# Moving half of an input projection's weight loads out of the key/value stage

## The reference, cut to what matters

```python
h = rms_norm(x, g_in)
proj = h @ w_in                      # w_in: 1024 x 3008, the weights that this change moves
c_q, c_kv, k_pe, z_a, cb, cc, cx, z_c = split(proj, [256, 128, 64, 512, 512, 512, 512, 512])
q  = rms_norm(rms_norm(c_q, g_cq) @ w_uq, g_q)         # 4 heads of 128 + 64 (rotary)
kv = rms_norm(c_kv, g_ckv) @ w_ukv                     # keys and values, 8192 rows
o_attn = causal_block_attention(q, k, v)
y_attn = rms_norm(o_attn * silu(z_a), g_oa)
u = causal_depthwise_conv(cc * cx, conv_w)             # three taps
y_conv = rms_norm(cb * u * silu(z_c), g_oc)
x = x + concatenate([y_attn, y_conv]) @ w_o
return x + sigmoid(rms_norm(x, g_pl) @ w_plg) * (p_i @ w_pl)
```

## Time and profile before

| | |
|---|---|
| time, median of 2 runs | 1702.0 us (1700.94 to 1703.05) |
| profiled execution: its time | 1699.79 us |
| profiled execution: span of the slowest core (core 4) | 1698.3 us |
| spans of the 8 cores | 1692.3 to 1698.3 us |
| mean granted TensorE clock of the cores | 0.814 to 0.822 of full speed |
| key/value stage on core 4 | about 60 to 338 us |
| iteration m = 0, from its first load to the start of attention | about 338 to 454 us |

### The profile page before, as it was taken

One profiled execution on the slowest core, in us unless ns is written; L12 is line 12 of the kernel. 1 busy time (PEld: TensorE's weight loads), 2 busy tenths in 40 slices (PEclk: granted clock), 3 DMA queues, 4 the chain that ended last, 5 costly groups with the idle time before them and its releaser, 6 DMA issues.

```text
span 1698.3 us, 22578 instructions; the slowest of 8 cores (1692.3 to 1698.3 us)
## 1 busy us (share of the span) xinstructions
PE 1101.1 (65%) x5973; PEld 572.1 (34%) x6060; DVE 952.5 (56%) x1560; ACT 964.3 (57%) x1668; POOL 89.8 (5%) x144
## 2 busy tenths in 40 slices
PE   0254556454786743898674478887764488988775
PEld 0243445322443321444332242333332243333332
DVE  5476777546662326477332557777223657777632
ACT  0465577542583434388444437887444258988644
POOL 1023233300000000000000000000000000000000
PEclk9967677665887866899796789998886589999888
DMA  2556554010241110000012000000111000000011
GB/s 68 159 188 222 185 180 141 17 48 0 77 147 57 43 62 1 1 1 1 32 57 74 1 1 1 1 1 25 35 41 62 1 1 1 1 1 1 32 41 40
DMA packets 27148, 87.05 MB, mean 51 GB/s; under 512 B 4464, under 2 KB 7792, under 8 KB 27024
## 3 DMA queue, kind: packets, MB, share of 16 engines
q1 hardware_dynamic: 27024, 85.61, 15.1%
HBM read 77.21 MB, written 8.39 MB: 50 GB/s over the span
## 4 chain that ended last, share of the span: by engine, by line
DVE 31%; PE 27%; ACT 19%; issue 14%; DMA 6%; DVEq 1%; ACTq 1%; SPq 1%; POOL 0%; POOLq 0%
PE bk L382 24%; DVE racc L352 15%; ACT pt L349 5%; DMA xt<-x_kv 3%; PE bk L389 3%; ACT gt L349 2%; DMA xo<-x_own 2%; ACT e L349 2%; DVEq L157 1%; DVE ssqkn L379 1%; ACT sjk L349 1%; ACT x1b L349 1%; DVE sq L352 1%; ACT sj L349 1%; ACT sqj L349 1%
## 5 line engine op out<-in xcount | busy, mean ns | idle before, releaser
L349 ACT ACTIVATE pt<-bk,zerob,rstdk 128x512 bf16<-128x512 f32 (+3 forms) x640 | 432.5, 716 | 67.5 <-PE bk L382 22.9
L352 DVE TENSOR_TENSOR racc<-racc,pt 128x512 f32<-128x512 f32 (+3 forms) x624 | 380.6, 610 | 114.2 <-DVE racc L352 59.0
L382 PE MATMUL bk<-pt,Vp 128*128 128x512 bf16 (+3 forms) x629 | 221.5, 352 | 56.6 <-ACT pt L349 46.3
L382 PE MATMUL bk<-QrT,KrT 128*128 128x512 bf16 (+3 forms) x634 | 230.4, 363 | 1.7 <-issue 0.8
L382 PE MATMUL bk<-QpT,KcT 128*128 128x512 bf16 (+3 forms) x621 | 224.5, 362 | 4.9 <-ACT rbc L349 3.7
L382 PEld LDWEIGHTS bk<-pt,Vp 128*128 128x128 bf16 x640 | 62.4, 97 | 232.4 <-issue 224.6
L382 PE MATMUL bk<-xTh,w_own 128*128 128x260 bf16 (+1 forms) x768 | 122.1, 324 | 5.8 <-ACT ccs L367 4.2
L382 PEld LDWEIGHTS bk<-xTh,w_own 128*128 128x128 bf16 x768 | 78.6, 103 | 48.9 <-issue 9.0
L382 PE MATMUL bk<-w_o,idb 128*128 128x512 bf16 x244 | 87.7, 519 | 2.0 <-issue 1.8
L349 ACT ACTIVATE sqj<-xt 128x1024 bf16<-128x1024 f32 x64 | 67.3, 1052 | 34.4 <-DMA xt<-x_kv 30.9
L382 PEld LDWEIGHTS bk<-QrT,KrT 128*128 128x128 bf16 x640 | 63.7, 100 | 65.6 <-issue 9.8
(11 more groups left out here) (189 smaller groups left out, 1662.5 us busy)
## 6 DMA issues: line engine op xcount, KB each, us to landing
xt<-x_kv SPq DMA_DIRECT2D x64, 512.0 KB, 4.8
xo<-x_own SPq DMA_DIRECT2D x16, 512.0 KB, 4.3
xr<-x_own SPq DMA_DIRECT2D x16, 512.0 KB, 4.2
out_own<-outst SPq DMA_DIRECT2D x16, 512.0 KB, 3.0
wst<-w_in SPq DMA_DIRECT2D x8, 752.0 KB, 6.3
wst_b<-w_in SPq DMA_DIRECT2D x8, 752.0 KB, 5.4
wst<-w_o SPq DMA_DIRECT2D x8, 512.0 KB, 4.1
wst<-w_plg SPq DMA_DIRECT2D x8, 512.0 KB, 4.0
```

The lines of the kernel that those rows point to most:

```text
L349: return S.op("act", lambda e: e.activation(**kw), reads, writes, sig)
L352: return S.op(eng, lambda e: e.tensor_tensor(out=out_, in0=in0, in1=in1, op=op), reads, writes)
L382: return S.op("pe", lambda e: e.matmul(out_, lhsT=lhsT, rhs=rhs, start=start, stop=stop), reads, writes, sig)
```

## The change

The second-half job of each of the 8 chunks leaves `job_list` for a list `late_jobs`. `job_list` keeps 10 jobs. In iteration m = 0 one staging buffer `wl` (128 x 1504, f32) is allocated ahead of the x buffers. The first late load is issued before the x loads of that iteration. After that each `late_consume` scales one job into `w_own` on DVE and issues the next load into the same `wl`. Two are consumed before `rope_tables`, three after A1b, and three after A1.

```diff
+    late_jobs = []
...
-        job_list.append((rows[:, 1504:3008], 1504, [(w_own[:, c, 1312:2816], 0, 1504)], g_in_pp[:, c:c + 1]))
+        late_jobs.append((rows[:, 1504:3008], 1504, [(w_own[:, c, 1312:2816], 0, 1504)], g_in_pp[:, c:c + 1]))
...
+        if m == 0:
+            wl = A("wl", [128, 1504], F32)
+            sl_wl = S.slot("wl")
+            late_state = dict(k=0)
+            def late_issue():
+                k = late_state["k"]
+                if k < len(late_jobs):
+                    src_ap, ncols, pieces, gain_ap = late_jobs[k]
+                    S.dma(lambda e: e.dma_start(out=wl[:, 0:ncols], in_=src_ap), sl_wl, (), [wl])
+            def late_consume():
+                k = late_state["k"]
+                if k >= len(late_jobs):
+                    return
+                src_ap, ncols, pieces, gain_ap = late_jobs[k]
+                for dst, lo, hi in pieces:
+                    ts("dve", dst, wl[:, lo:hi], gain_ap, None, ALU.mult, None, [wl, gain_src], [wdst_buf])
+                late_state["k"] = k + 1
+                late_issue()
+            late_issue()
...
         if m == 0:
+            late_consume()
+            late_consume()
             rope_tables(poso_i, 16, cosQ, sinQ)
...
         run_pipelined([cq_chain()] + [za_tile(s) for s in range(4)], skew=2, maxlive=3)
         AR.release(mQ1)
+        if m == 0:
+            for _ in range(3):
+                late_consume()
...
         AR.release(mQ)
+        if m == 0:
+            while late_state["k"] < len(late_jobs):
+                late_consume()
+        AR.release(m_wl)
```

More of the change, by code:

```diff
@@ L741, in build_program @@
         xTh = A("xTh", [128, 8, 4, 130], BF16)
+        m_wl = AR.mark()
+        if m == 0:
[17 more added lines that the diff above has]
+            late_issue()
         mL1 = AR.mark()
```

## The result

| | before | after |
|---|---|---|
| time, median | 1701.9 us (6 runs) | 1723.3 us (7 runs) |
| ratio | 1 | 1.0126, 95% interval 1.0112 to 1.0140 |
| profiled execution, slowest span | 1698.3 us | 1719.5 us (its time 1721.0) |

What follows compares the result with a forecast made beforehand. No engine fills the span, so an edit counts in its own stage: 8.6 + 14.7 + 12.4 = 35.7 us lost, 12.2 gained, +23.5 on 1699.8; with the median 2.2 higher, 1725 us, range 1715 to 1735.

Steps and rivals of the forecast that it cites:

- Part 1: Key/value stage: eight jobs leave, so four loaded rounds become rounds without weight loads; 12.2 us gained.
- Part 2: Start of m = 0: the first late load, issued ahead of the x loads, delays the first x tile by 2.0 us.
- Part 3: Late loads in m = 0: 5.45 us for each of five consumes that wait, 1.1 for each of three that do not.
- Groups: Late consumes in m = 0 before rotary tables, between gates and queries, and ahead of the convolution: 6.6, 14.7, 12.4 us lost.
- group 1: Two consumes before the rotary tables: delays by DVE's list and by the shared wdst_buf shift alike; 6.6 us lost.
- group 2: Three consumes between gate and query tiles: 12.0 us on DVE plus lost overlap of the query matmuls; 14.7 us.
- What costs nothing: Granted clock, SP's queue behind the late loads, and iterations 1 to 3: no loss claimed.
- The sum: Whole kernel: 35.7 us lost in m = 0, 12.2 gained in the key/value stage, +23.5.
- contended landings (1): Late loads land slower as all 8 cores ask for the same w_in rows; at 5.6 us each, 1732 us; chance 0.14.
- half the gain (2): Key/value rounds held near 17.9 us by something other than weights; half the gain 1731 us, none 1737; chance 0.08.
- landings of 3.8 (4): Faster landings in m = 0 and x tile delayed by 1: 3.5 us less; with upper gain, 1719 us; chance 0.10.
- cover (3): Waits in m = 0 run beside PE's and ACT's work: 1700 to 1701 us, no slower; chance 0.03.

Runs made afterwards that it cites:

- second traces: The kernel before and the changed kernel, each executed again unchanged; key/value stage 278.7 us before, 264.4 us after.
- e1b_no_late: Changed kernel without the eight late loads and their scalings, that part of w_own filled with a constant by ACT at the start; 1690.3 us, ratio 0.9937.
- e2_load_only: Kernel before with all loads, second halves scaled for only 16 of 1504 columns, the rest filled by POOL in setup; 1712.4 us, ratio 1.0090.
- e3_scale_only: Kernel before with all scalings, but seven of the eight second-half loads left out; 1696.8 us, ratio 0.9972.
- e6_after_x: Changed kernel with the first late load issued after the first two x loads of m = 0; 1719.4 us, ratio 1.0133.
- e4_own_buf: Changed kernel with late halves recorded as their own buffer, read only by conv_chunk's matmuls; DVE's list the same; 1720.4 us, ratio 1.0115.
- e7_pool: Changed kernel with four staging buffers, loads behind the second x load, scalings on POOL, own buffer read only by conv_chunk; 1724.4 us.

## Why the prediction was right

**Part 1** (12.2 us gained): 12.1 on the mean of the cores between the two traces (276.2 to 264.1), 11.1 in the start of m = 0 on core 4. Agreement to 0.1 us is luck, as the second traces give 14.3 (278.7 to 264.4) and e1b_no_late 9.3. The arithmetic of whole rounds was right, also in where the last round that issues a w_in load falls (141 us). The reason given for it was too simple: x queued behind the weights was to end the last wait and the scalings to be the rest, but taking away either alone brings back a small part, and the gain comes when both go (e2_load_only, e3_scale_only and the table of rounds).

**Part 2** (2.0): 2.1, and e6_after_x takes 1.8 of it back by the place alone.

**Part 3** (5.45 us for a waiting load): core 4's five waits of 4.8 us and scalings of 1.0 make 5.8. The median of the landings was right (4.3), but the five that count took 4.5 on the mean (+0.2), and the two hand-overs 0.25, with 0.55 once (0.1 assumed); the scaling was 0.04 shorter. The term is mis-sized by 0.35. The prediction's estimate from the Trainium skill, "DMA: Bandwidth & Descriptors", Specifications and Anatomy of one DMA, 4.15 us, is at the lower edge of the 4.1 to 5.0 measured on core 4. The 258 kB by which it extrapolated from the x load mix two units, as 770 kB less 512 KB is 246 kB; that is still 0.6 us.

**Groups** (6.6, 14.7, 12.4): 7.0, 14.8, 13.0. The step that claimed both ways through group 1 shift alike, and the lost overlap of 2.9 us in group 2, are confirmed by e4_own_buf, which took back 2.8 in group 2 and nothing in group 1.

**What costs nothing**: 1.4 us in fact. Gates, queries and convolution are each 0.35 to 0.65 us longer than in the first trace of before; the gates' share is within what untouched kernels show. On core 4 the clock looks as said; the kernel after in windows, the granted clock third from the end:

```profile
427.70:440.00 12.30, 0.00 (x0) 0.00 (x0) 2.95 (x4) 0.58 (x1) 0.00 (x0) 0.50 0.41 125
440.00:444.00 4.00, 3.96 (x19) 2.82 (x20) 0.15 (x1) 0.38 (x1) 0.00 (x0) 0.50 0.00 0
444.00:450.00 6.00, 6.00 (x41) 4.14 (x40) 2.93 (x6) 0.75 (x2) 0.00 (x0) 0.90 0.01 3
```

The convolution's first 4 us run at 1.2 GHz, as before. Over the eight cores it is not quite so. In the kernel before, where PE's query matmuls ran up to the convolution, the granted clock rose 3.5 us after the first matmul (1.9 to 5.2; 3.3 in the second trace). In the kernel after, where PE had stood still for 12 us, it rose 5.1 us after it (4.4 to 5.6; 4.6 in the second trace), and from that matmul to ycT it is 41.6 us instead of 40.7. So the pause took some 0.9 us by the clock, a term that the prediction put at nothing from one core's row.

**The sum** (+23.5): on the mean of the cores attention starts 25.8 us later, 2.3 more than the sum (37 lost in the parts named, 1.4 beside them, 12.3 gained). The total of +21.4 lies 2.1 below it, because 4.5 us came back after the start of attention, which the prediction had called unchanged; it had no row for that. That the time came within 2 us of 1725 is in part luck, two misses of opposite sign.

**Rivals**: contended landings (1) did not come, though all cores load the same rows at once (median 4.3 us on all cores, single ones to 5.5); half the gain (2) did not either, nor landings of 3.8 (4); cover (3) was nowhere, in e4_own_buf least of all, where the false waits were gone and the loss stayed.

## What to carry to other kernels

Moving a load out of a busy stage gains what that stage pays for it, but the load must be issued well ahead of its use where it goes: with one buffer behind its own consumer, each costs landing plus work on the engine that waits. Look at what stands behind the waiting instruction in its engine's list rather than at who waits longest: here the longest wait in the profile was worth a fifth of itself. And choose the engine for the moved work by its gaps and by whom it disturbs, not by how idle it is: POOL was idle and cost 27 us, ACT had gaps and cost nothing.

## What the runs showed of the hardware

An operation on POOL can hold up DVE for its whole length: a cast of 1.23 us took 11.04 under an 11.20 us fill on POOL, and in e7_pool casts and a scaling of 0.43 us took 4.1, one POOL instruction each, and some two-input operations of 0.69 us took 3.6. ACT's scalings of the same size disturbed nobody. The last iteration, with identical instructions, has two lengths 3.5 us apart that go with the granted TensorE clock (0.87 and 0.85). After a pause of 12 us on PE the granted clock rose to 1.00 5.1 us after the first matmul of the convolution, without the pause after 3.5 us, on the mean of the cores.
